# Pre-norm gain vectors moved from the activations into the weight splits

## The reference

```
def rms_norm(x, g):
    y = x * rsqrt(mean(x * x, axis=-1) + EPS)
    return y * g
f = swiglu(rms_norm(x, g[0]), w_gate, w_up, w_down)
x = x + 0.5 * rms_norm(f, g[1])
h = rms_norm(x, g[2])
k, v = split(rms_norm(x, g_kv) @ w_kv)
```

## Time and profile before

| | value |
|---|---|
| median of three runs | 1594.97 us |
| span of the profiled execution | 1595.4 us |
| TensorE busy with matmuls | 1435.1 us, 90% of the span |
| VectorE busy | 828.5 us, 52% |
| ScalarE busy | 675.1 us, 42% |
| mean granted TensorE clock | 0.941 |
| HBM read | 245.3 MB, 154 GB/s over the span |

### The profile page before, as it was taken

The page is one execution under the profiler, slowest core; times in us unless marked ns, Lnnn a source line. Parts: engine busy times, 40 slices in busy tenths (PEclk is TensorE's granted clock), DMA queues, the critical chain, the costliest instruction groups (busy, mean ns, idle before and its releaser), DMA issues.

```text
span 1595.4 us, 17161 instructions
## 1 busy us (share of the span) xinstructions
PE 1435.1 (90%) x6508; PEld 1171.2 (73%) x6508; DVE 828.5 (52%) x880; ACT 675.1 (42%) x792; POOL 40.9 (3%) x95
## 2 busy tenths in 40 slices
PE   5999989689999889999876899998999968799996
PEld 3888868468888677888664678886787747688884
DVE  2554454645544545544548554455667174555542
ACT  3444353334443533444345354443652263254431
POOL 1000010000000100000000000000000000000000
PEclk9999999799999999999986899999999977899998
DMA  5755636126556226555520245563544311455540
GB/s 165 246 181 193 221 101 241 49 100 211 184 185 233 100 101 211 184 185 196 210 102 17 80 162 192 198 210 132 211 159 134 106 53 53 148 196 184 184 145 27
DMA packets 160137, 247.03 MB, mean 155 GB/s; under 512 B 8991, under 2 KB 104409, under 8 KB 160089
## 3 DMA queue, kind: packets, MB, share of 16 engines
q1 hardware_dynamic: 159808, 246.28, 45.1%
q10 hardware_dynamic: 280, 0.10, 0.0%
HBM read 245.30 MB, written 1.05 MB: 154 GB/s over the span
## 4 chain that ended last, share of the span: by engine, by line
PE 83%; DVE 10%; ACT 4%; issue 2%; POOL 0%; POOLq 0%; DVEq 0%; ACTq 0%
PE GU L473 16%; PE GU L474 15%; PE GU L475 15%; PE DD L473 10%; PE DD L475 10%; PE DD L474 10%; DVE wlo L1289 3%; PE TB L505 2%; ACT whi L923 2%; PE TB L602 2%; DVE tmp L1407 1%; PE DD L779 1%; DVE x L1413 1%; DVE sm L1475 1%; ACT junk L947 1%
## 5 line engine op out<-in xcount | busy, mean ns | idle before, releaser
L1289 DVE TENSOR_TENSOR wlo<-raw,whi 128x2048 fp32r<-128x2048 f32 (+1 forms) x226 | 512.4, 2282 | 321.2 <-ACT whi L923 321.2
L923 ACT ACTIVATE whi<-raw 128x2048 fp32r<-128x2048 f32 (+1 forms) x226 | 427.4, 1904 | 203.9 <-PE DD L475 191.5
L473 PE MATMUL GU<-whi,xh 128*128 128x512 f32 (+1 forms) x1088 | 438.9, 403 | 10.7 <-DVE wlo L1289 4.6
L474 PE MATMUL GU<-wlo,xh 128*128 128x512 f32 (+1 forms) x1088 | 429.9, 395 | 0.0
L475 PE MATMUL GU<-whi,xl 128*128 128x512 f32 (+1 forms) x1088 | 429.8, 395 | 0.0
L473 PEld LDWEIGHTS GU<-whi,xh 128*128 128x128 f32 x1088 | 210.4, 193 | 55.0 <-issue 9.8
L475 PEld LDWEIGHTS GU<-whi,xl 128*128 128x128 f32 x1088 | 209.0, 192 | 45.0
L474 PEld LDWEIGHTS GU<-wlo,xh 128*128 128x128 f32 x1088 | 209.8, 193 | 41.2
L473 PE MATMUL DD<-whi,hth 128*128 128x512 f32 x480 | 188.1, 392 | 9.8 <-DVE htl L1350 9.8
L474 PE MATMUL DD<-wlo,hth 128*128 128x512 f32 x480 | 187.3, 390 | 0.0
L475 PE MATMUL DD<-whi,htl 128*128 128x512 f32 x480 | 187.2, 390 | 0.0
(11 more groups left out here) (250 smaller groups left out, 947.8 us busy)
## 6 DMA issues: line engine op xcount, KB each, us to landing
raw<-in_w_ffn_gate SPq DMA_DIRECT2D x88, 512.0 KB, 3.7
raw<-in_w_ffn_up SPq DMA_DIRECT2D x88, 512.0 KB, 4.7
raw<-in_w_ffn_down SPq DMA_DIRECT2D x88, 512.0 KB, 4.1
raw<-in_w_ff SPq DMA_DIRECT2D x64, 512.0 KB, 4.3
raw<-in_w_in SPq DMA_DIRECT2D x40, 512.0 KB, 4.4
raw<-in_w_conv_in SPq DMA_DIRECT2D x24, 512.0 KB, 4.7
raw<-in_w_kv SPq DMA_DIRECT2D x16, 512.0 KB, 4.8
raw<-in_w_conv_out SPq DMA_DIRECT2D x8, 512.0 KB, 4.3
```

What stands on the lines that cost most here:

```text
L473: pe.matmul(dst, h, w_h, start=start, stop=False)
L474: pe.matmul(dst, h, w_l, start=False, stop=False)
L923: nc.scalar.activation(whi[s][:, 0:size], raw[s][:, 0:size], ACT.Copy).then_inc(hi_done[s], 1)
L1289: nc.vector.tensor_tensor(wlo[s][:, 0:size], raw[s][:, 0:size], whi[s][:, 0:size].bitcast(F32), ALU.subtract).then_inc(lo_done[s], 1)
```

## The change

The gain is no longer applied to x. Each entry of a product that follows a pre-norm carries `gain`, the index of its first column in `col1`. Its split is then made k-tile by k-tile: ScalarE issues four instructions of 512 columns with the gain as their scale in place of one of 2048 columns, and VectorE four `scalar_tensor_tensor` in place of one `tensor_tensor`. 150 of the 226 splits are of this kind. The others (second matrices of the feed-forwards, conv_out, o, the branches, w_out) stay.

The split of x has no gain any more and covers two k-tiles with one instruction of 512 columns. pre3 and pre4 now have the same split x, so the second one (16 transposes and their copies) is left out.

```diff
@@ plan @@
-    def linear(name, w, allow=4):
+    def linear(name, w, gain=None, allow=4):
...
-                st.add(pair[0] * 2 + half, 4, m, two(w[:, 4 * half:4 * half + 4, c:c + m], 4))
+                st.add(pair[0] * 2 + half, 4, m, two(w[:, 4 * half:4 * half + 4, c:c + m], 4),
+                       gain=None if gain is None else gain + 4 * half)
...
-    linear("kv", a["w_kv"])
-    ffn("ffn2", 1, 0)
-    linear("q", a["w_q"][0])
+    linear("kv", a["w_kv"], R_GKV)
+    ffn("ffn2", 1, 0, 48)
+    linear("q", a["w_q"][0], 64)
@@ TensorE @@
             prep(ktok)
-            prep(x, defer=True)
             ffn("ffn2")
@@ ScalarE, split @@
-                    nc.scalar.activation(whi[s][:, 0:size], raw[s][:, 0:size], ACT.Copy).then_inc(hi_done[s], 1)
+                    if e.gain is None:
+                        nc.scalar.activation(whi[s][:, 0:size], raw[s][:, 0:size], ACT.Copy).then_inc(hi_done[s], 1)
+                    else:
+                        for k in range(e.kt):
+                            ks = slice(k * e.cols, (k + 1) * e.cols)
+                            ins = nc.scalar.activation(whi[s][:, ks], raw[s][:, ks], ACT.Copy,
+                                                       scale=col1[:, e.gain + k:e.gain + k + 1])
+                        ins.then_inc(hi_done[s], 1)
@@ ScalarE, prep @@
-                    for j in range(2):
-                        ins = nc.scalar.activation(xh[:, 2 * b + j, :], TB[:, bank, j * S:(j + 1) * S], ACT.Copy,
-                                                   scale=cols(2 * b + j))
-                    ins.then_inc(xh_done, 1)
+                    nc.scalar.activation(xh[:, 2 * b:2 * b + 2, :].rearrange("p k n -> p (k n)"), TB[:, bank, :], ACT.Copy)\
+                        .then_inc(xh_done, 1)
@@ ScalarE, prep_x @@
-                prep(PRE[name])
                 if fresh:
+                    prep()
@@ VectorE, split @@
-                    nc.vector.tensor_tensor(wlo[s][:, 0:size], raw[s][:, 0:size], whi[s][:, 0:size].bitcast(F32),
-                                            ALU.subtract).then_inc(lo_done[s], 1)
+                        for k in range(e.kt):
+                            ks = slice(k * e.cols, (k + 1) * e.cols)
+                            ins = nc.vector.scalar_tensor_tensor(
+                                out=wlo[s][:, ks], in0=raw[s][:, ks], scalar=col1[:, e.gain + k:e.gain + k + 1],
+                                in1=whi[s][:, ks].bitcast(F32), op0=ALU.mult, op1=ALU.subtract)
+                        ins.then_inc(lo_done[s], 1)
@@ VectorE, prep @@
-                    for j in range(2):
-                        k = 2 * b + j
-                        ins = nc.vector.scalar_tensor_tensor(
-                            out=xl[:, k, :], in0=TB[:, bank, j * S:(j + 1) * S], scalar=cols(k),
-                            in1=xh[:, k, :].bitcast(F32), op0=ALU.mult, op1=ALU.subtract)
-                    ins.then_inc(t_used[bank], 1)
+                    nc.vector.tensor_tensor(xl[:, ks, :].rearrange("p k n -> p (k n)"), TB[:, bank, :],
+                                            xh[:, ks, :].rearrange("p k n -> p (k n)").bitcast(F32), ALU.subtract)\
+                        .then_inc(t_used[bank], 1)
```

More of the change, by code:

```diff
@@ L55, with __init__ @@
 class Entry:
-    def __init__(self, slot, raw_before, split_before, kt, cols, split, pieces, step):
-        self.step = step
+    def __init__(self, slot, raw_before, split_before, kt, cols, split, pieces, step, gain):
+        self.step, self.gain = step, gain
         self.slot, self.raw_before, self.split_before = slot, raw_before, split_before
@@ L73, in start, with add @@
         self.segment[name], self.allow[name] = len(self.entries), allow
-    def add(self, slot, kt, cols, pieces, split=True, step=0):
-        self.entries.append(Entry(slot, self.raw[slot], self.split[slot], kt, cols, split, pieces, step))
+    def add(self, slot, kt, cols, pieces, split=True, step=0, gain=None):
+        self.entries.append(Entry(slot, self.raw[slot], self.split[slot], kt, cols, split, pieces, step, gain))
         self.raw[slot] += 1
@@ L101, in linear, with ffn @@
             for half in range(2):
-                st.add(pair[0] * 2 + half, 4, m, two(w[:, 4 * half:4 * half + 4, c:c + m], 4))
+                st.add(pair[0] * 2 + half, 4, m, two(w[:, 4 * half:4 * half + 4, c:c + m], 4),
+                       gain=None if gain is None else gain + 4 * half)
             pair[0] ^= 1
-    def ffn(name, layer, which):
+    def ffn(name, layer, which, gain):
         st.start(name, 2)
@@ L114, in first @@
                     (slice(0, 4), slice(0, FG), lambda i, ks=ks: gate[:, ks, bass.ds(i * FG, FG)]),
-                    (slice(0, 4), slice(FG, 512), lambda i, ks=ks: up[:, ks, bass.ds(i * FG, FG)])], step=g)
+                    (slice(0, 4), slice(FG, 512), lambda i, ks=ks: up[:, ks, bass.ds(i * FG, FG)])], step=g, gain=gain + 4 * half)
         def second(g):
@@ L136, in first @@
                     (slice(k, k + 2), None, lambda i, k=k, half=half: w1[:, 4 * half + k:4 * half + k + 2, bass.ds(i * 512, 512)])
-                    for k in (0, 2)], step=g)
+                    for k in (0, 2)], step=g, gain=R_N2 + 4 * half)
         def second(g):
@@ L149, in ff @@
         second(STEPS2 - 1)
-    ffn("ffn0", 0, 0)
-    linear("conv_in", a["w_conv_in"][0])
+    ffn("ffn0", 0, 0, 0)
+    linear("conv_in", a["w_conv_in"][0], 16)
     linear("conv_out", a["w_conv_out"][0])
-    ffn("ffn1", 0, 1)
-    linear("kv", a["w_kv"])
-    ffn("ffn2", 1, 0)
-    linear("q", a["w_q"][0])
+    ffn("ffn1", 0, 1, 32)
+    linear("kv", a["w_kv"], R_GKV)
+    ffn("ffn2", 1, 0, 48)
+    linear("q", a["w_q"][0], 64)
     linear("o", a["w_o"][0])
-    ffn("ffn3", 1, 1)
-    linear("w_in", a["w_in_2"][0])
+    ffn("ffn3", 1, 1, 80)
+    linear("w_in", a["w_in_2"][0], R_N1)
     st.start("cmp", 4)
@@ L263, in rcol @@
             return rs[:, c:c + 1]
[L265 to L270, removed]
         def P3(lo, n, base=0, width=N_IN):
@@ L928, in split_to, with prep @@
                     n.next += 1
-            def prep(cols, kts=KT):
-                for b in range(kts // 2):
+            def prep():
+                for b in range(KT // 2):
                     bank = b % 2
@@ L1288, in split @@
                     dve.wait_ge(hi_done[s], d + e.split_before + 1)
-                    nc.vector.tensor_tensor(wlo[s][:, 0:size], raw[s][:, 0:size], whi[s][:, 0:size].bitcast(F32),
-                                            ALU.subtract).then_inc(lo_done[s], 1)
+                    if e.gain is None:
+                        nc.vector.tensor_tensor(wlo[s][:, 0:size], raw[s][:, 0:size], whi[s][:, 0:size].bitcast(F32),
+                                                ALU.subtract).then_inc(lo_done[s], 1)
+                    else:
+                        for k in range(e.kt):
[4 more added lines that the diff above has]
+                        ins.then_inc(lo_done[s], 1)
             def split_to(i):
@@ L1302, in prep @@
                     dve.wait_ge(xh_done, n.xh)
-                    for j in range(2):
-                        k = 2 * b + j
-                        ins = nc.vector.scalar_tensor_tensor(
-                            out=xl[:, k, :], in0=TB[:, bank, j * S:(j + 1) * S], scalar=cols(k),
-                            in1=xh[:, k, :].bitcast(F32), op0=ALU.mult, op1=ALU.subtract)
-                    ins.then_inc(t_used[bank], 1)
+                    ks = slice(2 * b, 2 * b + 2)
+                    nc.vector.tensor_tensor(xl[:, ks, :].rearrange("p k n -> p (k n)"), TB[:, bank, :],
+                                            xh[:, ks, :].rearrange("p k n -> p (k n)").bitcast(F32), ALU.subtract)\
+                        .then_inc(t_used[bank], 1)
             def prep_x(name, then):
                 split_to(seg[then] + (1 if then == "ffn0" else 2))
-                prep(PRE[name])
+                if name != "pre4":
+                    prep()
                 split_to(seg[then] + st.allow[then])
```

## The result

The kernel is slower. The median of four runs is 1605.06 us (1603.26 to 1605.97) against 1594.97 before, ratio 1.0058 with the interval 1.0045 to 1.0071. A second comparison (e9, in the last group of experiments) gives 1.0051, 1.0037 to 1.0064, with medians 7.0 us apart. So the change costs 7 to 10 us, where the forecast had 6.4 and 1601.4 us in a range of 1597.3 to 1605.0. The median of the first comparison lies at the upper edge of that range, 0.06 us outside; 1.0058 times 1594.97 is 1604.2, inside.

What follows compares the result with a forecast made beforehand. TensorE bounds the kernel, so splits cost only where it waits. Terms 1.77 + 4.40 + 0.90 - 3.17 + 0.68 + 0.92 + 0.86 = +6.4 us, forecast 1601.4 us; own range 1598.5 to 1604.5, overall range 1597.3 to 1605.0.

Steps and rivals of the forecast that it cites:

- Prices: New instructions of 512 columns: 0.725 us on ScalarE, 748 ns on VectorE; four cost 0.66 and 0.43 us more.
- Rival 4: VectorE's new instruction runs at half throughput, +32 us on the path, 1633 us; chance 0.02.
- rival 3: Short instructions in a row have next to no cost of their own, prices at lower bounds, 1591.7 us; chance 0.06.
- Loops: Feed-forward loops: 14.5 us more on ScalarE and 9.5 on VectorE, hidden by TensorE's 182.46 us; cost 0.
- Start: Two TensorE waits at the kernel's start grow by 0.91 and 0.86 us, together +1.77.
- the four entries: conv_in, kv, q, w_in behind a feed-forward: x queues behind longer splits, +1.10 us each, +4.40 for four.
- rival 2: Splits ahead of `post` don't gate it; the entries give -0.41 instead of +1.10 us each, 1595.4 us; chance 0.10.
- ffn2: With x's split shared, TensorE waits for the first `wlo` alone, and four transposes go: -3.17 us.
- ffn1, ffn3, ff: Step 1 waits for `hid` at ffn1 and ffn3, +0.45 us each; w_out's addition to x waits at ff, +0.68.
- rival 1: The clock falls once more in w_in, behind a wait grown from 1.67 to 2.6 us; 1603.1 us; chance 0.14.
- the groups behind the entries: Groups of conv_in, kv, q, most of w_in: 5.3 us of VectorE beside about 11 us of TensorE; cost 0.
- the bounds: The same sum with all prices at their lower bounds is -3.3 us, at their upper ones +15.

Runs made afterwards that it cites:

- e9: The changed kernel run again without an edit, against the kernel before: 1603.36 us, ratio 1.0051.
- e3: The changed kernel without the gain column, still four instructions of 512 columns for each pre-norm entry: 1591.77 us, ratio 0.9974 to the kernel before.
- e4: The changed kernel without gains and with every weight split whole again, x split unscaled and shared: 1587.21 us, ratio 0.9944 to the kernel before.
- e7: The changed kernel with the split of the next stage's second entry moved behind x: 1588.01 us, ratio 0.9954 to the kernel before.
- e8: The kernel before with the split of the next stage's second entry moved behind x: 1583.37 us, ratio 0.991.
- e10: The kernel before with one x split for kv and ffn2, only ffn2's weights scaled, by the ratio of the two gains: 1593.31 us, ratio 0.9979.
- e1: The changed kernel with the second split of x, for ffn2, put back: 1608.25 us, ratio 1.0076 to the kernel before.
- e2: The kernel before with gains folded only into the weights of kv and ffn2, which share one split of x: 1594.15 us, ratio 0.9993.
- e11: e10 with the split of the next stage's second entry moved behind x: 1578.45 us, ratio 0.9888 to the kernel before.

## Why the prediction held, and what it left out

1. Prices. The duration of the new instructions was built from neighbours, the same operation from SBUF with a column scalar. It was off by 13 and 2 ns. The rule of the Trainium skill on VectorE's throughput (Vector Engine (DVE) Microarchitecture Reference, Points that are easy to get wrong) does not show in the trace: 746 ns a row, where a plain subtraction of the same shape takes 686 in e3. Rival 4 fell with it, and rival 3 with the 712 ns. For ScalarE the Trainium skill (ScalarE: Activation LUTs, What ACT_TABLE_LOAD costs) gives 186 ns plus 0.833 a column, 93 more for a column operand, and 93 of overlap between neighbours. Worked out that is an estimate of 706 ns for one and 2.54 us for four; the trace has 712 ns and 2.55 us and agrees.
2. Loops. Cost 0 was right: 170.1 us in both, with VectorE at 53% of the stretch.
3. Start and the four entries. +1.77 and +4.40 were predicted, +1.79 and +4.49 found. e3 and e4 show the two steps of the entry's wait, e7 and e8 that the splits ahead of `post` set it, and rival 2 falls.
4. ffn2. -3.17 against -3.18, and e10 has it alone with 3.1 to 3.4 us. e1 shows it by its absence.
5. ffn1, ffn3, ff. Mis-sized by 1.7 us together: 1.58 predicted, 3.28 found. At ffn1 the wait for x grew by 0.38 us, which I had counted as untouched. At ff I had priced the wait ahead of x alone. It grew by 1.09, as 0.66 + 0.43 says, but step 1, which had waited 0.82 us for `sg`, now waits 1.13 for the third entry's `wlo`, and part of the step ran at the lower clock.
6. The clock. This is the term that was missing. I let it fall once more in w_in, behind the wait for `hid` (rival 1). The trace has that wait at 2.55 us, and the stretch behind it grew by nothing but the 0.88 of the next wait. So rival 1's 1603.1 is nearer to the measured time than the forecast, but at the wrong place. It was behind the entries that more clock was lost: at three of the four TensorE stayed longer at 1.2 GHz, 3.1 us in this profile. "Cost 0" for the groups behind the entries was right for the splits and wrong for the clock. That the longer wait is the cause is not shown. Of the 13 waits of 6.2 us at entries in the traces of after, e9, e1 and e2, ten have 13.8 to 14.4 us from the start of the wait to the first matmul at 0.4 us and three have 11.7 to 11.9; for the waits of 3.5 to 5.4 us at the four entries, in before, e2, e3, e4, e7, e8, e10 and e11, it is 10.4 to 12.9. Within these it does not grow with the wait.
7. The sum. The waits of the profile make +8.1 and the clock behind the entries +3.0, 11.1 us. The pair of traces gives 4.9 of it back where the change did little. The medians are 10.1 and 7.0 us apart. So the profile pair's +6.1 fits the predicted +6.4 partly by luck: a sum of waits that was 1.7 too low, and two shares of the clock, +3.0 and -4.9, that it did not have. The prediction also took the span for the time of the profiled execution; since it added 6.4 to the median in the end, that moved nothing.
8. The range. 1598.5 to 1604.5 is not what its reason gives: half the distance to the bounds (-3.3 and +15 for 6.4) would be 1596.5 to 1605.7. That would have held 1605.06.

Open stays how the 7 to 10 us divide. Between runs of the same kernel the mean clock moves from 0.939 to 0.941 or from 0.940 to 0.943 and the time by up to 5 us, which is as much as the term in question. Why q's entry shows no longer stretch at the lower clock, with the same wait, is also open. It isn't something about q: in e1, where q comes 4.4 us later, the wait is the same 6.2 us and the stretch behind it is 1.2 us longer than in after.

## What to carry to other kernels

A scale that moves from the activation to the weights turns one long instruction into one for each group of 128 rows. Price it where a split stands ahead of something that TensorE waits for (here 1.1 us a split) and not in the loops. Fold it only where it saves a pass, and only into the weights that need it: the ratio of two gains for one consumer kept the 3.2 us and avoided the cost; it needs a gain that is never zero. Before adding to work ahead of a wait, ask whether that work needs to be there at all. Moving the second split behind x was worth 13 to 17 us, more than anything that the change dealt with.

## What was not expected of the hardware

- What a wait costs in clock does not follow its length. Three entries lost another 1.0 us behind a wait that was 1.55 us longer, and the fourth nothing. In e2 kv's entry with 6.20 us of wait lost nothing more, and behind the 3.48 us of e8 the matmuls were slow for longer (7.7 us) than behind the 4.66 of before (6.8).
- A stretch without any edit changes its time with the clock that it is granted: attention took 81.2 to 84.1 us in these traces, at a mean of 0.81 to 0.75.
- Matmuls of no use in the waits raise the mean clock from 0.941 to 0.956 and are worth 13.5 us of 1596, with the rest of the kernel untouched.
- The same kernel is granted different clocks in different executions. One run of e8 took 1574.41 us at a mean clock of 0.954, where its median is 1583.37. A difference of a few us needs many runs, and a profile's span has to be set beside the time of that same execution.
